# Input stage: high parts read from PSUM, a norm from token rows, and one matmul for all relative-position rows

## The reference

```
h = rms_norm(x, gla_norm)            # x * rsqrt(mean(x*x) + eps) * g
proj = h @ gla_w_in                  # q, k, v, r, g_low; k (gk), v (gv), q (gq), r (gr) in 2048 -> 6160 columns
log_a = log_sigmoid(g_low @ w_gate_up + b_gate) / 16
... chunked linear attention, * silu(r), @ gla_w_out, residual, squared-relu MLP, norm
... second block: attention with
s_own = q k^T / sqrt(128) + rel_table[t5_bucket(dist)]     # 8 heads, 32 buckets, dist = q_pos - k_pos
... LRU and short-convolution branches, gates, MLP, final norm
```

## Time and profile before

| | us |
|---|---|
| median of 3 runs | 2713.06 |
| lowest and highest | 2712.98, 2714.33 |
| profiled execution | 2713.99 |
| its span on the core | 2711.9 |
| TensorE, weight loads | 2685.3, 2361.2 |
| VectorE, ScalarE, GpSimd | 1796.7, 1352.0, 86.7 |

### The profile page before, as it was taken

One profiled execution on the slowest core, in us unless ns is written; L12 is line 12 of the kernel. 1 busy time (PEld: TensorE's weight loads), 2 busy tenths in 40 slices (PEclk: granted clock), 3 DMA queues, 4 the chain that ended last, 5 costly groups with the idle time before them and its releaser, 6 DMA issues.

```text
span 2711.9 us, 43584 instructions
## 1 busy us (share of the span) xinstructions
PE 2685.3 (99%) x15627; PEld 2361.2 (87%) x15627; DVE 1796.7 (66%) x2074; ACT 1352.0 (50%) x1628; POOL 86.7 (3%) x69
## 2 busy tenths in 40 slices
PE   8999999999999999999999999999999999999998
PEld 6888888888888888888888888888888888888887
DVE  6666767656666567866786666666676566665664
ACT  4546555444444445544675554554554444444443
POOL 3000010000000001200000000000000000000001
PEclk9999999999999999999999999999999999999999
DMA  6564556666566666665556555555556666666653
GB/s 184 163 202 132 179 190 189 196 193 193 191 192 197 194 187 194 193 210 179 164 160 198 183 190 186 187 190 187 186 186 194 194 194 193 189 195 196 194 186 132
DMA packets 507075, 504.45 MB, mean 186 GB/s; under 512 B 17732, under 2 KB 505433, under 8 KB 506985
## 3 DMA queue, kind: packets, MB, share of 16 engines
q1 hardware_dynamic: 505820, 501.60, 59.1%
q10 hardware_dynamic: 1164, 1.63, 0.2%
HBM read 499.50 MB, written 3.67 MB: 186 GB/s over the span
## 4 chain that ended last, share of the span: by engine, by line
PE 96%; DVE 2%; issue 1%; ACT 1%; POOL 0%; DVEq 0%; POOLq 0%; ACTq 0%
PE acc L491 59%; PE acc L493 30%; PE acc L486 3%; PE acc L488 2%; DVE wsp L1030 1%; DVE lat L1311 0%; PE misc L591 0%; PE misc L606 0%; PE misc L710 0%; PE misc L548 0%; ACT wsp L764 0%; POOL ssq L447 0%; PE misc L507 0%; DVE z L1038 0%; PE misc L573 0%
## 5 line engine op out<-in xcount | busy, mean ns | idle before, releaser
L1030 DVE TENSOR_TENSOR wsp<-raw,wsp 128x1024 fp32r<-128x1024 f32 x944 | 1167.4, 1244 | 584.0 <-ACT wsp L764 559.2
L491 PE MATMUL acc<-xs,wsp 128*128 128x512 f32 x4224 | 1468.4, 394 | 9.4 <-DVE wsp L1030 9.3
L764 ACT ACTIVATE wsp<-raw 128x1024 fp32r<-128x1024 f32 x944 | 995.0, 1059 | 693.9 <-PE acc L493 632.6
L493 PE MATMUL acc<-xs,wsp 128*128 128x256 f32 x4224 | 1177.8, 279 | 0.0
L491 PEld LDWEIGHTS acc<-xs,wsp 128*128 128x128 f32 x4224 | 794.6, 188 | 184.3 <-DVE wsp L1030 11.3
L491 PE MATMUL acc<-hs,wsp 128*128 128x512 f32 x2560 | 879.6, 391 | 0.0
L493 PEld LDWEIGHTS acc<-xs,wsp 128*128 128x128 f32 x4224 | 798.5, 189 | 0.4
L493 PE MATMUL acc<-hs,wsp 128*128 128x256 f32 x2560 | 710.1, 277 | 0.0
L491 PEld LDWEIGHTS acc<-hs,wsp 128*128 128x128 f32 x2560 | 480.6, 188 | 102.0
L493 PEld LDWEIGHTS acc<-hs,wsp 128*128 128x128 f32 x2560 | 481.8, 188 | 0.0
L773 ACT ACTIVATE corr<-acc 128x512 f32<-128x512 f32 x248 | 148.8, 600 | 408.0 <-PE acc L493 389.0
(11 more groups left out here) (213 smaller groups left out, 1016.2 us busy)
## 6 DMA issues: line engine op xcount, KB each, us to landing
raw<-in_w_in SPq DMA_DIRECT2D x224, 512.0 KB, 4.2
raw<-in_mlp_w_up SPq DMA_DIRECT2D x128, 512.0 KB, 3.9
raw<-in_mlp_w_down SPq DMA_DIRECT2D x128, 512.0 KB, 3.9
raw<-in_w_mlp_up SPq DMA_DIRECT2D x128, 512.0 KB, 4.0
raw<-in_w_mlp_down SPq DMA_DIRECT2D x128, 512.0 KB, 4.3
raw<-in_gla_w_in SPq DMA_DIRECT2D x96, 512.0 KB, 3.8
raw<-in_gla_w_out SPq DMA_DIRECT2D x32, 512.0 KB, 4.1
raw<-in_w_out SPq DMA_DIRECT2D x32, 512.0 KB, 4.1
```

The source lines that it names most:

```text
L491: pe.matmul(acc[:, g, j], w_part(0, slot)[:, t, cols], x[:, k0 + k], start=start, stop=False, skip_group_check=True)
L493: ins = pe.matmul(acc[:, g, j, 1], w_part(1, slot)[:, t, cols], x[:, k0 + k, 0], start=False, stop=stop, skip_group_check=True)
L764: act.activation(w_part(0, slot), raw[:, slot], ACT.Copy).then_inc(hi_done, 1)
L1030: dve.tensor_tensor(w_part(1, slot), raw[:, slot], w_part(0, slot).bitcast(F32), ALU.subtract).then_inc(lo_done, 1)
```

## The change

It edits the first stage, the norm of the first block and the bias rows.

- **Loads.** x's quarters and the four loads of block gk 0 alternate. The loads of block gk 1 follow `wg_raw`, each with four of the parameter vectors behind it, then `wgu`.
- **Pairs.** `M[i % 4]` is used for the transposes, six pairs ahead of the first unit and two ahead of the second. ScalarE reads the PSUM tile with the gain as scale and writes the high part; VectorE does gain multiply and subtraction in one instruction from the same tile. The copy to `xres` is VectorE's for even pairs and ScalarE's for odd ones.
- **Norm.** ScalarE squares each token row of `xtok` with a running sum (`xsum`), takes the root; VectorE inverts it (`rcol`) and multiplies the unit matrix by it; two matmuls of ones with this diagonal give `rstd`. They stand behind block gk 1, with the parameter transposes. GpSimd's sums of the first norm and the transposes of `rstd` are gone, and block gk 0 is scaled after block gk 1's norm (`first_keys`).
- **Bias rows.** One matmul with `table` itself gives all 8 heads in 8 partitions. Eight transfers write a head each to `bias_scratch`, every one reading its partition 128 times, at the ends of gv 1 to gv 7 and gq 0.

The core of the diff (left out: allocations, semaphore names and counts, GpSimd's loop, which now skips the first norm, and VectorE's copies for `rcol` and `tbc`, which are taken out):

```diff
@@ -355,18 +357,25 @@
                 load(w, UK * P * u, col, rnd, u)
 
 
+        def parameters(names):
+            for name in names:
+                r, k = ROWS[name]
+                sp.dma_start(stage[r % P:r % P + k, r // P], a[name].rearrange("(r p) -> r p", p=P)).then_inc(par_landed, 16)
+
         for q in range(4):
             cols = slice(q * UK * P, (q + 1) * UK * P)
             sp.dma_start(xtok[:, :, cols], a["x"][:, cols].rearrange("(j p) n -> p j n", p=P)).then_inc(x_landed[q], 16)
-        block_load(a["gla_w_in"], KEYW, 0)
+            load(a["gla_w_in"], UK * P * q, KEYW, 0, q)
         sp.dma_start(wg_raw[:], a["gla_w_in"][:, 2 * KEYW + 2 * VALW:].rearrange("(t p) n -> p t n", p=P)
                      ).then_inc(wg_landed, 16)
+        others = list(ROWS)[1:]
+        for u in range(4):
+            load(a["gla_w_in"], UK * P * u, KEYW + NB, 1, u)
+            parameters(others[4 * u:4 * u + 4])
         sp.dma_start(wgu[:], a["gla_w_gate_up"]).then_inc(wg_landed, 16)
-        for name, (r, k) in list(ROWS.items())[1:]:
-            sp.dma_start(stage[r % P:r % P + k, r // P], a[name].rearrange("(r p) -> r p", p=P)).then_inc(par_landed, 16)
 
         def straight(name, i, b, rnd, g):
-            if (name, i) == ("gk", 0):
+            if name == "gk" and i < 2:
                 return
             w, col = w_cols[name]
             block_load(a[w], col + i * NB, rnd)
...
@@ -519,51 +528,55 @@
 
         def inputs(u):
 
-            for i in ((0, 1, 2, 3, 4), (5, 6), (7,), ())[u]:
+            for i in ((0, 1, 2, 3, 4, 5), (6, 7), (), ())[u]:
                 if i % 2 == 0:
                     pe.wait_ge(x_landed[i // 2], 16)
-                if i >= 3:
-                    pe.wait_ge(value_ready, i - 2)
+                if i == 3:
+                    pe.wait_ge(par_done, 1)
+                if i >= 4:
+                    pe.wait_ge(split_done, i - 3)
+                    if i % 2 == 0:
+                        pe.wait_ge(x_kept, i // 2 - 1)
                 for t in range(2):
                     for j in range(TT):
                         k = 2 * i + t
-                        ins = pe.transpose(M[i % 3][:, t, j * P:(j + 1) * P], xtok[:, j, k * P:(k + 1) * P], ident[:])
+                        ins = pe.transpose(M[i % 4][:, t, j * P:(j + 1) * P], xtok[:, j, k * P:(k + 1) * P], ident[:])
                 ins.then_inc(x_mm, 1)
-            if u == 3:
-
-                pe.wait_ge(par_landed, 16 * (len(ROWS) - 1))
-                pe.wait_ge(par_done, 1)
-                pe.transpose(M[3][:, 0, 0:ROWS_A], stage[0:ROWS_A, 0], ident[0:ROWS_A, 0:ROWS_A])
-                pe.transpose(M[3][:, 1, 0:ROWS_B], stage[0:ROWS_B, 1], ident[0:ROWS_B, 0:ROWS_B]).then_inc(par_mm, 1)
+
+        def first_norm():
+
+            pe.wait_ge(diag_ready, 1)
+            pe.wait_ge(x_kept, 4)
+            pe.wait_ge(const_done, 2)
+            for j in range(TT):
+                ins = pe.matmul(M[0][:, 0, j * P:(j + 1) * P], ones[:], h[:, 0, j * P:(j + 1) * P], start=True, stop=True,
+                                skip_group_check=True)
+            ins.then_inc(norm_mm, 1)
+
+            pe.wait_ge(par_landed, 16 * (len(ROWS) - 1))
+            pe.wait_ge(split_done, PAIRS)
+            pe.transpose(M[3][:, 0, 0:ROWS_A], stage[0:ROWS_A, 0], ident[0:ROWS_A, 0:ROWS_A])
+            pe.transpose(M[3][:, 1, 0:ROWS_B], stage[0:ROWS_B, 1], ident[0:ROWS_B, 0:ROWS_B]).then_inc(par_mm, 1)
 
         def hooks(name, i):
-            if name == "gv":
-
-                pe.wait_ge(table_ready, 1)
-                if i:
-                    pe.wait_ge(bias_copied, i)
-                else:
-                    pe.wait_ge(gate_min, 2)
-                    pe.wait_ge(gate_abs, 2)
-                pe.matmul(flat[3][:, 0:BW], tbc[:, i], onehot[:], start=True, stop=True).then_inc(bias_mm, 1)
+            if (name, i) == ("gv", 0):
+
+                pe.wait_ge(zero_done, 3)
+                pe.wait_ge(tab_landed, 32)
+                pe.wait_ge(gate_min, 2)
+                pe.wait_ge(gate_abs, 2)
+                pe.matmul(flat[3][0:AH, 0:BW], table[:], onehot[:], start=True, stop=True).then_inc(bias_mm, 1)
             if (name, i) == ("gk", 1):
 
                 pe.wait_ge(wg_ready, 1)
-                pe.wait_ge(std_done, 1)
                 for k in range(KT):
                     pe.matmul(M[1], wgs[:, k, 0], xs[:, k], start=(k == 0), stop=False, skip_group_check=True)
                     ins = pe.matmul(M[1][:, 1], wgs[:, k, 1], xs[:, k, 0], start=False, stop=(k == KT - 1),
                                     skip_group_check=True)
                 ins.then_inc(glow_mm, 1)
-
-                pe.wait_ge(rstd_done, 1)
-                for j in range(TT):
-                    ins = pe.transpose(M[2][:, j, 0:P], rstd[:, j * P:(j + 1) * P], ident[:])
-                ins.then_inc(rcol_mm, 1)
             if name == "gk" and i in (2, 3):
 
                 pe.wait_ge(glow_done, 1)
-                pe.wait_ge(rcol_done, 1)
                 pe.wait_ge(par_done, 2)
                 if i == 3:
                     pe.wait_ge(gate_min, 1)
...
@@ -805,21 +819,46 @@
                 act.activation(rtmp[:], rstd[:], ACT.Sqrt, scale=1.0 / D, bias=cst[:, 0:1]).then_inc(std_done, 1)
 
         act.dma_start(stage[0:KT, 0], a["gla_norm"].rearrange("(r p) -> r p", p=P)).then_inc(gain_landed, 16)
+        act.wait_ge(par_done, 1)
         for i in range(PAIRS):
-            emit(PAIR0["x1"] + i, xs, i, src=(h, fo)[i % 2])
-            squares(0, i)
+            act.wait_ge(x_mm, i + 1)
+            for j in range(2):
+                ins = act.activation(xs[:, 2 * i + j, 0], M[i % 4][:, j], ACT.Copy, scale=prm("gla_norm", 2 * i + j))
+            if i % 2 == 1:
+                ins = act.activation(xres[:, 2 * i:2 * i + 2], M[i % 4], ACT.Copy)
+            ins.then_inc(hi_ready, 1)
             if i % 2 == 1:
                 split_hi(0, i // 2)
         act.wait_ge(const_done, 4)
 
+        def first_evac(g):
+
+            def token_squares(j):
+                for q in range(4):
+                    act.wait_ge(x_landed[q], 16)
+                own.done(act.activation(xsquare[:], xtok[:, j], ACT.Square, accum_out=xsum[:, j:j + 1]))
+
+            split_hi(1, 0)
+            split_hi(1, 1)
+            token_squares(0)
+            split_hi(1, 2)
+            token_squares(1)
+            split_hi(1, 3)
+            act.activation(rcol[:], xsum[:], ACT.Sqrt, scale=1.0 / D, bias=cst[:, 0:1]).then_inc(std_done, 1)
+            act.wait_ge(unit_used, SLOTS)
+            act.activation(corr[:, g], acc[:, g, :, 1], ACT.Copy).then_inc(corr_ready, 1)
+
         def gla_hooks(name, i):
-            if name == "gv":
-                act.wait_ge(bias_mm, i + 1)
-                act.activation(bias_rows[:, i], flat[3][:, 0:BW], ACT.Copy).then_inc(bias_copied, 1)
-            if (name, i) == ("gq", 0):
-
-                act.wait_ge(bias_copied, AH)
-                act.dma_start(scratch.rearrange("(h p n) -> p h n", h=AH, p=P), bias_rows[:]).then_inc(bias_out, 16)
+            if (name, i) == ("gv", 0):
+                act.wait_ge(bias_mm, 1)
+                act.activation(bias_rows[:], flat[3][0:AH, 0:BW], ACT.Copy).then_inc(bias_copied, 1)
+            block = {"gv": i, "gq": 8 + i}.get(name, 0)
+            if 1 <= block <= AH:
+
+                hd = block - 1
+                act.wait_ge(bias_copied, 1)
+                act.dma_start(scratch[hd * P * BW:(hd + 1) * P * BW].rearrange("(h p n) -> h p n", h=1, p=P),
+                              bias_rows[hd:hd + 1].unsqueeze(1).to_broadcast([1, P, BW])).then_inc(bias_out, 16)
             if (name, i) == ("gk", 0):
                 act.wait_ge(wg_landed, 32)
                 act.wait_ge(zero_done, 1)
...
@@ -875,13 +914,14 @@
                 ins.then_inc(o_copied, 1)
 
         def gla(name, i, b, rnd, g):
-            evac(b, rnd, 0, 4, g)
             if (name, i) == ("gk", 0):
-                std(0)
+                first_evac(g)
+            else:
+                evac(b, rnd, 0, 4, g)
             if name == "gr":
                 function(FUN0["gr"] + i, ACT.Sigmoid)
                 if i == 0:
-                    act.wait_ge(bias_out, 16)
+                    act.wait_ge(bias_out, 16 * AH)
                 emit(PAIR0["gr"] + i, hs, i)
             gla_hooks(name, i)
 
...
@@ -1062,17 +1104,38 @@
         dve.wait_ge(par_mm, 1)
         dve.tensor_copy(par[:, 0:KT], M[3][:, 0, 0:KT]).then_inc(par_done, 1)
         dve.wait_ge(par_done, 1)
-        for i in range(PAIRS + 1):
-            if i < PAIRS:
-                dve.wait_ge(x_mm, i + 1)
-                dve.tensor_copy(xres[:, 2 * i:2 * i + 2], M[i % 3])
-                for j in range(2):
-                    ins = dve.tensor_scalar((h, fo)[i % 2][:, j], M[i % 3][:, j], prm("gla_norm", 2 * i + j), None, ALU.mult)
-                ins.then_inc(value_ready, 1)
-            if i:
```

(41 more changed lines are left out.)

67 lines of the change are left out of this document (32 added, 35 removed).

## The result

| | before | after |
|---|---|---|
| median, us | 2713.12 (4 runs) | 2740.40 (4 runs) |
| lowest and highest | 2712.98, 2714.33 | 2739.13, 2741.13 |
| span of the profiled execution | 2711.9 | 2739.3 |

The changed kernel is slower: 1.0099 times the time before, 95% interval 1.0082 to 1.0117. That is 27.3 us more, where 15.6 less were forecast.

The account below looks back on a forecast made before the run. The prediction took TensorE, busy 99% of the span, to bound the kernel. Gains of 8.2 us (first stage) and 7.3 (relative-position rows) sum to 15.5, taking the median from 2713.06 to 2697.5 us; range 2694 to 2702.5.

Parts of the forecast that it names:

- First stage: Start of the kernel: TensorE's waits for weight splits go, block gk 2 starts at 44.65 instead of 52.84; gain 8.2 us.
- (1): First stage stays tight on ScalarE, TensorE waits and may drop its clock: 2699.5 to 2701.5 us; chance 0.18.
- (4): Interleaved loads delay x's third quarter, first unit at 14 or later: 2698.5 to 2699; within the forecast's 0.62.
- the first unit: First matmul unit of block gk 0, kept at the low clock: 4.38 us, starting at 13.3.
- the transposes behind it: Block gk 0, between the first two units: eight transposes at full clock, 1.0 us.
- Relative-position matmuls: Between blocks from gv on: seven of eight 384-column matmuls go, 1.04 us each; gain 7.3 us.
- Row transfers: Eight bias-row writes at block ends, gv to gq: taken as hidden behind TensorE, cost zero.
- my own sign of being wrong: In gv: forecast wrong if blocks are over 11.3 us apart, or if block gk 2 starts later than 46.
- Rival (2): Row transfers hold queue engines x us each, weights late: loss 8 (x - 5.7) - 5; chance 0.07, beyond 10 us 0.03.
- so what starts earlier at 52.84 (block gk 2, the third) ends earlier by as much: From block gk 2 on: TensorE has no gap until the output, so the 8.2 us gain carries to the end.

Follow-up runs that it names:

- e4: The changed kernel with xsum allocated behind all other tiles, so every old tile keeps its place; 2720.26 us (8 runs), one at 2698.51.
- h1: The kernel before with the new input stage alone, all small tiles in their old places; 2704.58 us (5 runs), one at 2724.91.
- g3: e4 with the relative-position rows written once, by one transfer in place of eight; 2717.50 us (10 runs).
- e3: The kernel before with an unused 32-byte tile that shifts the small tiles behind it, ones included; 2753.30 us (2 runs), ratio 1.0143.
- f1: The kernel before with 64 unused bytes behind rcol; 2751.54 us (4 runs).
- f2: The kernel before with the matrix of ones moved by 32 bytes and what lies behind it by 64; 2752.12 us (4 runs).
- f3: The kernel before with all small tiles moved by 32, 64 or 96 bytes, the ones by 64; 2752.18 us (4 runs).
- h4: g3 with the first MLP's norm matmuls in pieces of 128 columns; 2696.76 us (4 runs), ratio 0.9935 to the kernel before.

## Why the prediction was wrong

**First stage: right.** Every start within 0.2 us, block gk 2 at 44.63 for 44.65. Rivals (1) and (4) did not come. One term was off, and two others made up for it: the first unit took 4.71 us (13.15 to 17.86), not 4.38, but it began 0.15 earlier, and the transposes behind it took 0.79 (17.86 to 18.65), not 1.0. That it came out to 0.02 us is luck. In the twelve traces with the new first stage block gk 2 starts between 42.6 (e4) and 44.6 (after); seven of them start it before 43.7, where the gain is over 9.1 us. They differ in how long the first unit takes and in the pitch of the first blocks, 340 in e4 and 350 in after.

**Relative-position matmuls: right.** Seven matmuls less are worth 7.3 us in gv (97.07 less 89.80), as forecast. By the norm of the first MLP, h1 has gained 9.2 us and g3, which has both parts and one transfer, 17.5 (431.26 - 413.77); the forecast had 15.5, and most of the rest is the first stage (9.7 in g3).

**Row transfers: the term was mis-sized.** I took zero; they cost 3.6 us in after. By that my own sign of being wrong came, gv blocks over 11.3 apart: from 70.94 to 164.32 they are 11.67 apart in after, and 11.22 in g3. Rival (2) was right in its mechanism (x = 8.9, late raw tiles between 100 and 180), but its formula gives 8 x (8.9 - 5.7) - 5 = 20.6 at that x. Wrong in it was to count a transfer's landing time as time in which all engines are held: even in the 20 us with the stall the core moved 158 GB/s, against 206 without the eight, and nearly every late tile was covered by the split ahead of TensorE.

The Trainium skill, page "SBUF — State Buffer", section "Door 1: The DMA port swizzle", gave an estimated 7.1 us for such a transfer; the trace has 8.9, 22 GB/s. The page was a better guide than the nearest row of my own.

**What failed** is the step "so what starts earlier at 52.84 (block gk 2, the third) ends earlier by as much". It holds only if a pair costs the same afterwards. I had read one pitch, 0.347 to 0.35, off the first stage and gv, and never looked at the MLPs, which are half of the run; there a pair takes 340 ns. The profile of before had two pitches for one and the same instruction, within the first 80 us too, and I should have asked what holds the faster one up. The account closes: 8.2 us gained in the first stage and 7.3 in the relative-position matmuls, 3.6 lost to the transfers, 38.8 to the pitch of the MLPs, together 26.9 more, where the spans differ by 27.4. What sets the pitch stays open. None of my rivals had this, so the chance of 0.95 for faster rested on the edits alone.

**At equal pitch the edits do about what was forecast.** Both MLPs at 350: 2740.4 against 2751.5 to 2753.3 (e3, f1, f2, f3), 11 to 13 us faster, with the eight transfers in it; the forecast was 15.6, and 12 with the 3.6 for them. Both at 340: h4's 2696.8 against 2713.6, 16.9 faster, with one transfer.

## What to carry to other kernels

Look for stretches in which the same instruction has different periods under a busy engine, by counting its instructions in windows of equal length: where the base is in the faster one, any edit may lose it, and 32 unused bytes in the base are a cheap test of that. Judge an edit at equal pitch, or against several layouts of the base, before it is kept or thrown away. Do not add landing times of narrow transfers as if they closed the queue; look at the rate that the other loads keep.
